# A three-product float32 transformer trunk: shorter GpSimd subtractions, moved diagonals, and VectorE's low halves in four operations

## What is computed

```python
for i in range(2):
    x = layer_norm(ALPHA * x + 0.5 * swiglu(x, ffn1_w_gu[i], ffn1_w_down[i]), ...)
    if i == 0: y, qm = gla_mix(x @ gla_w_in, ...);   w_out = gla_w_out
    else:      y, qm = conv_mix(x @ conv_w_in, ...); w_out = conv_w_out
    m = mem_attention(qm, mem, mem_w_kv[i])
    x = layer_norm(ALPHA * x + concatenate([y, m]) @ w_out, ...)
    x = layer_norm(ALPHA * x + 0.5 * swiglu(x, ffn2_w_gu[i], ffn2_w_down[i]), ...)
```

## Time and profile before

| | |
|---|---|
| median of 3 runs | 2048.76 us (2047.93 to 2050.04) |
| the profiled execution | 2046.01 us |
| its span, first to last instruction | 2044.3 us |
| TensorE busy / weight loads | 99% / 91% of the span |
| VectorE, ScalarE, GpSimd busy | 67%, 40%, 39% |
| granted TensorE clock, mean | 0.998 |
| HBM traffic | 215.8 MB read, 22.0 MB written, 116 GB/s |
| GpSimd, first feed-forward block | busy 8 to 9 tenths of slices 3 and 4 of 40 |

### The profile page before, as it was taken

One profiled execution on the slowest core, in us unless ns is written; L12 is line 12 of the kernel. 1 busy time (PEld: TensorE's weight loads), 2 busy tenths in 40 slices (PEclk: granted clock), 3 DMA queues, 4 the chain that ended last, 5 costly groups with the idle time before them and its releaser, 6 DMA issues.

```text
span 2044.3 us, 34286 instructions
## 1 busy us (share of the span) xinstructions
PE 2019.4 (99%) x13509; PEld 1853.8 (91%) x13509; DVE 1364.4 (67%) x1843; ACT 810.5 (40%) x1164; POOL 789.2 (39%) x444
## 2 busy tenths in 40 slices
PE   9999999999999999999999999999999899999998
PEld 9899998988988999999899999889887699999887
DVE  4477774554435768887456887646899886776645
ACT  5433452263433354444234444423453434434422
POOL 1499820033312258881015878001100335887000
PEclk9999999999999999999999999999999999999999
DMA  7545323332211234443232545233544322332232
GB/s 251 186 144 164 124 88 98 105 105 77 69 32 62 93 114 150 158 155 109 93 107 93 165 146 172 96 96 108 177 128 169 103 73 94 103 103 92 90 102 88
DMA packets 229513, 239.13 MB, mean 117 GB/s; under 512 B 5999, under 2 KB 222189, under 8 KB 227628
## 3 DMA queue, kind: packets, MB, share of 16 engines
q1 hardware_dynamic: 228780, 235.68, 35.4%
q10 hardware_dynamic: 640, 2.16, 0.3%
HBM read 215.80 MB, written 22.02 MB: 116 GB/s over the span
## 4 chain that ended last, share of the span: by engine, by line
PE 86%; POOL 4%; DVE 4%; issue 3%; ACT 2%; DMA 1%; DVEq 0%; SPq 0%; ACTq 0%; POOLq 0%
PE bank L1779 12%; PE bank L1780 12%; PE bank L1781 12%; PE bank L1908 10%; PE bank L1910 10%; PE bank L1909 10%; PE bank L1790 4%; PE bank L1791 4%; PE bank L1792 4%; PE bank L1862 1%; ACT whi L669 1%; POOL s L557 1%; POOL diag_tmp L589 1%; PE bank L1867 1%; PE bank L2210 1%
## 5 line engine op out<-in xcount | busy, mean ns | idle before, releaser
L669 ACT CAST whi<-raw 128x2048 fp32r<-128x2048 f32 (+3 forms) x191 | 324.0, 1697 | 875.2 <-POOL scratch L564 435.5
L1123 DVE TENSOR_TENSOR wlo<-raw,whi 128x2048 fp32r<-128x2048 f32 (+2 forms) x165 | 356.0, 2157 | 244.7 <-ACT whi L669 244.2
L541 POOL TENSOR_TENSOR tiny<-tiny 128x2 f32<-128x2 f32 (+1 forms) x13 | 9.4, 726 | 754.2 <-DVE tiny L1398 754.2
L560 POOL TENSOR_TENSOR raw<-raw 128x512 f32<-128x512 f32 x72 | 226.2, 3142 | 0.0
L1779 PE MATMUL bank<-h_hi,whi 128*128 128x512 f32 x528 | 207.1, 392 | 0.0
L1780 PE MATMUL bank<-h_lo,whi 128*128 128x512 f32 x528 | 205.5, 389 | 0.0
L1781 PE MATMUL bank<-h_hi,wlo 128*128 128x512 f32 x528 | 205.5, 389 | 0.0
L1908 PE MATMUL bank<-t_hi,whi 128*128 128x256 f32 x576 | 163.6, 284 | 2.8 <-DVE bank L1190 2.8
L564 POOL TENSOR_TENSOR scratch<-raw,s 128x512 f32<-128x512 f32 x72 | 149.2, 2073 | 39.7 <-DVE ex_lo L1130 39.7
L1908 PE MATMUL bank<-t_hi,ex_hi 128*128 128x256 f32 x576 | 163.8, 284 | 0.3 <-DVE ex_lo L1132 0.2
L1909 PE MATMUL bank<-xlo,whi 128*128 128x256 f32 x576 | 163.0, 283 | 0.0
(11 more groups left out here) (356 smaller groups left out, 5886.1 us busy)
## 6 DMA issues: line engine op xcount, KB each, us to landing
raw<-in_ffn_w_gu_dram SPq DMA_DIRECT2D x88, 1024.0 KB, 4.9
raw<-in_ffn_w_down_dram SPq DMA_DIRECT2D x32, 896.0 KB, 5.1
raw<-in_ffn_w_down_dram SPq DMA_DIRECT2D x32, 512.0 KB, 3.4
raw<-in_gla_w_in_dram SPq DMA_DIRECT2D x14, 1024.0 KB, 5.1
...
```

Of the source, the lines that this page charges most:

```text
L560: nc.gpsimd.tensor_tensor(a21, a21, a11, ALU.add).then_inc(w_sum, 1)
L669: nc.scalar.copy(whi[:, s, 0:kc, 0:width], raw[:, s, 0:kc, 0:width]).then_inc(hi_ready, 1)
L1123: nc.vector.tensor_tensor(wlo[:, s, 0:kc, 0:width], raw[:, s, 0:kc, 0:width], whi[:, s, 0:kc, 0:width].bitcast(F32), ALU.subtract).then_in ...
```

## The change

Five edits.
1. `lo_blocks`: GpSimd's subtractions outside the loops and weight sums (chunks GLA_N + 14 and + 15, the output projections' chunks, the spare parts, `b_lo_c`) go in blocks of 128x256, four or eight operations instead of one. In the convolution block two of the eight blocks of chunk CONV_OUT_N + 2 move ahead of `rsqrt`.
2. The diagonals: 0, 1, 2 ahead of the loop; 3, 4, 5 in passes 3, 5, 7; 6 and 7 behind it. SyncE's stores move accordingly, one between the two loads of a pass for passes 1 and 2. VectorE's wait for the stores moves to just before `residual_pair` of the first column pair.
3. The third memory chunk (n = 2) is cast and subtracted in two halves, and TensorE waits for each.
4. `r_evac(3)` goes ahead of `step(15)`.
5. In the first feed-forward block, passes 2 to 10, VectorE makes the low half of a full chunk in four operations of 128x512 back to back (`split_lo_quarters`); the semaphore counts after the last.

```diff
@@ -79,6 +79,7 @@
 GLU_EVAC = [2, 4, 6, 8, 14, 16, 18, 20]
 LATE = 3
 TAPS_K = [8, 8, 7, 7]
+DIAG_PAIR = [3, 5, 7]
 PE_TAPS = sum(TAPS_K)
 
 
...
@@ -342,13 +344,21 @@
...
                 n0 = FFN_N[f]
+
+                def diagonal_store(d):
+                    sp.wait_ge(diag_built, d + 1)
+                    sp.dma_start(diag_dram[d // 2, d % 2], diag_tmp[:, :, :].bitcast(F32)).then_inc(diag_stored, 16)
+
                 if f == 0:
                     for i in range(FK // 2):
                         load(n0 + 2 * i, 0, cols(w_gu, i * 256))
+                        if i in (1, 2):
+                            diagonal_store(2 * i - 2)
                         load(n0 + 2 * i + 1, 1, cols(w_gu, i * 256 + FF))
-                        if 0 < i <= 2 * len(TAPS_K):
-                            sp.wait_ge(diag_built, i)
-                            sp.dma_start(diag_dram[(i - 1) // 2, (i - 1) % 2], diag_tmp[:, :, :].bitcast(F32)).then_inc(diag_stored, 16)
+                        if i == 1:
+                            diagonal_store(1)
+                        if i - 1 in DIAG_PAIR:
+                            diagonal_store(3 + DIAG_PAIR.index(i - 1))
                 else:
                     def gate_and_up(i):
                         load(n0 + 2 * i, 0, cols(w_gu, i * 256))
@@ -387,7 +397,11 @@
                 if f in (1, 2):
                     sp.wait_ge(early_done, EARLY * f + 1)
                     early_store(EARLY - 1)
+                if f == 0:
+                    diagonal_store(6)
                 down_loads(0, (2, 3))
+                if f == 0:
+                    diagonal_store(7)
                 with sp.Fori(1, 4) as p:
                     down_loads(p, range(4))
 
@@ -510,6 +524,18 @@
 
         @block.gpsimd
         def _(pool):
+            def lo_blocks(to, whole, high, ks):
+                for k in ks:
+                    last = nc.gpsimd.tensor_tensor(to[:, k, :], whole[:, k, :], high[:, k, :].bitcast(F32), ALU.subtract)
+                return last
+
+            def split_lo_blocks(n, s, kc=8, after_dve=False):
+
+                pool.wait_ge(hi_ready, n + 1)
+                if after_dve:
+                    pool.wait_ge(lo_ready, n)
+                lo_blocks(wlo[:, s], raw[:, s], whi[:, s], range(kc)).then_inc(lo_ready, 1)
+
             def split_lo(n, s, kc=8, width=256, after_dve=False):
 
                 pool.wait_ge(hi_ready, n + 1)
@@ -524,8 +550,8 @@
                 for i in range(2):
                     pool.wait_ge(hi_ready, n0 + 4 + i + 1)
                     pool.wait_ge(lo_ready, n0 + 4 + i)
-                    nc.gpsimd.tensor_tensor(to[:, 1, A_K * i:A_K * i + A_K, :], raw[:, i, 0:A_K, :],
-                                            to[:, 0, A_K * i:A_K * i + A_K, :].bitcast(F32), ALU.subtract).then_inc(lo_ready, 1)
+                    lo_blocks(to[:, 1, A_K * i:A_K * i + A_K, :], raw[:, i], to[:, 0, A_K * i:A_K * i + A_K, :],
+                              range(A_K)).then_inc(lo_ready, 1)
 
             def lo_of(base, ks, tok, lo, hi):
                 for k in ks:
@@ -592,14 +618,16 @@
                         values[:, sum(TAPS_K[:g]):sum(TAPS_K[:g]) + kc, t:t + 1].to_broadcast([P, kc, P]), ALU.mult)
                 last.then_inc(diag_built, 1)
 
-            for i in range(PLAIN):
-                diagonal(i)
+            for d in range(3):
+                diagonal(d)
             pool.wait_ge(t_ready, 4)
             for i in range(PLAIN, FK // 2):
                 weight_sums(0, i, 0)
                 weight_sums(0, i, 1)
-                if i < 2 * len(TAPS_K):
-                    diagonal(i)
+                if i in DIAG_PAIR:
+                    diagonal(3 + DIAG_PAIR.index(i))
+            for d in (6, 7):
+                diagonal(d)
             norm(LN_FFN[0])
 
             nc.gpsimd.memset(att_mask, 1.0).then_inc(gla_masks, 1)
@@ -618,15 +646,15 @@
             with pool.Fori(1, 5) as i:
                 split_lo(GLA_N + 4 + 2 * i, 0)
                 split_lo(GLA_N + 5 + 2 * i, 1)
-            split_lo(GLA_N + 14, 0)
-            split_lo(GLA_N + 15, 1)
+            split_lo_blocks(GLA_N + 14, 0)
+            split_lo_blocks(GLA_N + 15, 1)
             pool.wait_ge(rms_var, 1)
             nc.gpsimd.tensor_tensor(rms_r, rms_v, minus_half, ALU.pow).then_inc(rms_rs, 1)
-            split_lo(GLA_OUT_N, 0, A_K)
-            split_lo(GLA_OUT_N + 1, 1, A_K)
-            split_lo(GLA_OUT_N + 3, 1, B_K, after_dve=True)
+            split_lo_blocks(GLA_OUT_N, 0, A_K)
+            split_lo_blocks(GLA_OUT_N + 1, 1, A_K)
+            split_lo_blocks(GLA_OUT_N + 3, 1, B_K, after_dve=True)
             spare_lo_parts(LN_GLA_OUT, GLA_OUT_N)
-            split_lo(GLA_OUT_N + 7, 1, B_K, after_dve=True)
+            split_lo_blocks(GLA_OUT_N + 7, 1, B_K, after_dve=True)
             norm(LN_GLA_OUT)
             all_weight_sums(1)
             norm(LN_FFN[1])
@@ -634,17 +662,20 @@
             norm(LN_FFN[2])
             nc.gpsimd.memset(conv_in[:, :, 0:PAD], 0.0).then_inc(conv_pad, 1)
 
+            pool.wait_ge(hi_ready, CONV_OUT_N + 3)
+            pool.wait_ge(lo_ready, CONV_OUT_N + 2)
+            lo_blocks(wlo[:, 0], raw[:, 0], whi[:, 0], range(2))
             rsqrt(LN_CONV, 0)
             pool.wait_ge(rstd_diag, UNIT[LN_CONV] + 1)
-            split_lo(CONV_OUT_N + 2, 0, B_K, after_dve=True)
+            lo_blocks(wlo[:, 0], raw[:, 0], whi[:, 0], range(2, B_K)).then_inc(lo_ready, 1)
             pool.wait_ge(raw_loaded[1], 16 * (CONV_OUT_N // 2 + 4))
             pool.wait_ge(mo_mm, 2 * HEADS)
             nc.gpsimd.tensor_copy(b_hi_c[:, :, :], raw[:, 1, :, :]).then_inc(b_hi_done, 1)
             pool.wait_ge(b_hi_done, 1)
             pool.wait_ge(w_used, DIAG_N + len(TAPS_K))
-            nc.gpsimd.tensor_tensor(b_lo_c[:, :, :], raw[:, 1, :, :], b_hi_c[:, :, :].bitcast(F32), ALU.subtract).then_inc(lo_ready, 1)
+            lo_blocks(b_lo_c, raw[:, 1], b_hi_c, range(8)).then_inc(lo_ready, 1)
             spare_lo_parts(LN_CONV_OUT, CONV_OUT_N)
-            split_lo(CONV_OUT_N + 7, 1, B_K, after_dve=True)
+            split_lo_blocks(CONV_OUT_N + 7, 1, B_K, after_dve=True)
             norm(LN_CONV_OUT)
             all_weight_sums(3)
             rsqrt(LN_FFN[3], 0)
@@ -898,7 +929,12 @@
             nc.scalar.copy(whi[:, 1, 4:8, :], raw[:, 1, 4:8, :]).then_inc(hi_ready, 1)
             for n in range(8):
                 act.wait_ge(w_used, n + 1)
-                split_hi(n // 2 + 1, n % 2)
+                if n == 0:
+                    act.wait_ge(raw_loaded[0], 32)
+                    nc.scalar.copy(whi[:, 0, 0:4, :], raw[:, 0, 0:4, :]).then_inc(third_hi, 1)
+                    nc.scalar.copy(whi[:, 0, 4:8, :], raw[:, 0, 4:8, :]).then_inc(hi_ready, 1)
+                else:
+                    split_hi(n // 2 + 1, n % 2)
                 for t in range(2):
                     c = n % 4
                     to = kv_t[:, n // 4, 2 * c + t, :] if c < 2 else kv_v[:, n // 4, t, (c - 2) * 256:(c - 1) * 256]
@@ -1017,9 +1053,12 @@
                 if h % 2 == 0:
                     step(12 + h // 2)
             for k in range(8):
-                if k in (0, 2):
-                    step(14 + k // 2, A_K)
-                    r_evac(2 + k // 2)
+                if k == 0:
+                    step(14, A_K)
+                    r_evac(2)
+                if k == 2:
+                    r_evac(3)
+                    step(15, A_K)
                 if k == 6:
                     split_hi(GLA_OUT_N // 2 + 1, 0, B_K)
                 act.wait_ge(y_ready, k + 1)
@@ -1123,6 +1162,15 @@
                 nc.vector.tensor_tensor(wlo[:, s, 0:kc, 0:width], raw[:, s, 0:kc, 0:width],
                                         whi[:, s, 0:kc, 0:width].bitcast(F32), ALU.subtract).then_inc(lo_ready, 1)
 
+            def split_lo_quarters(n, s):
+
+                dve.wait_ge(hi_ready, n + 1)
+                dve.wait_ge(lo_ready, n)
+                for k in range(0, 8, 2):
+                    last = nc.vector.tensor_tensor(wlo[:, s, k:k + 2, :], raw[:, s, k:k + 2, :],
+                                                   whi[:, s, k:k + 2, :].bitcast(F32), ALU.subtract)
+                last.then_inc(lo_ready, 1)
+
             def extra_lo(f, i, s):
 
                 q = summed(f, i, s)
@@ -1194,7 +1242,10 @@
                 n, last = FFN_N[f] + 2 * i, isinstance(i, int)
                 for step in range(3):
                     combine(f, i, 0, step)
-                split_lo(n + 1, 1)
+                if f == 0:
+                    split_lo_quarters(n + 1, 1)
+                else:
+                    split_lo(n + 1, 1)
                 combine(f, i, 0, 3)
                 extra_lo(f, i, 1)
                 if f in (1, 2):
@@ -1204,7 +1255,10 @@
                                             ALU.subtract).then_inc(early_done, 1)
                 for step in range(3):
                     combine(f, i, 1, step)
```

(26 more changed lines are left out.)

1 line of the change is left out of this document (added).

## The result

After: 2065.7 us median (2063.97 to 2068.68, 4 runs); before, on the same chip: 2049.4 us median (2047.93 to 2051.33, 4 runs). Ratio 1.0086, 95% interval 1.0074 to 1.0098: 0.9% slower. The profiled execution has a span of 2062.9 us against 2044.3.

The account below looks back on a forecast made before the run. TensorE's busy line (2019.4 of 2044.3 us) was taken as the bound. Terms 20.0 - 1.35 - 1.8 - 0.7 - 0.6 - 3.6 = +12.0 on 2046.0 gave 2058.0, plus 2.8 to the median: 2060.8 us, range 2044 to 2068.

Parts of the forecast that it names:

- Quarters: First feed-forward block: GpSimd's sums enter between VectorE's four operations, the load loop becomes the bound; net +20 us.
- steady halves: First feed-forward block, halves of a pass without diagonal or its store: nine cost 1.05 us each.
- disturbed half: First feed-forward block, half with a diagonal or its store: three sums enter; six cost 14.3 us together.
- diagonal 6 there costs nothing: Last pass of the first feed-forward loop: no sums left, so the low half still meets its deadline; 0 us.
- Rival A: First feed-forward block: VectorE keeps its turn through back to back quarters; faster, 2038.7 us; chance 0.14.
- Rival B: First feed-forward block: turns taken but loads come sooner; no change, some 2047 us; chance 0.14.
- x near zero: First feed-forward block: what GpSimd's operation still holds when VectorE's low half starts stays near zero.
- Waits behind L1242: TensorE's waits at 688 and 1650 us: VectorE no longer held behind GpSimd's long subtractions; -1.8 us.
- `c_lo`, variance: Convolution block: blocks end `c_lo` sooner, while two blocks ahead delay the variance steps; -3.6 us, bounds 0 and -6.2.
- `r_late`: `r_evac(3)` placed before the cast of 1.04 us removes TensorE's wait of 0.45 + 0.16; -0.6 us.
- kv chunk: Third memory chunk cast and subtracted in halves, so TensorE's idling for its low half goes; -1.35 us.
- stores: Diagonal stores moved on SyncE, possibly delaying load 13; 0 us, bounds 0 and +3.

Follow-up runs that it names:

- run 2: Kernel before, with only the quarters in the first feed-forward block added and six diagonals in the loop: 2076.6 us, ratio 1.0142.
- runs 3 and 4: Changed kernel: first, two low-half operations instead of four, 2054.8 us; second, quarters kept, GpSimd's third sum waiting for the low half in passes 3 to 10, 2052.1 us.
- run 6: Changed kernel without quarters, spare low parts and chunk before each output norm in one GpSimd operation in GLA and convolution blocks: 2043.5 us.
- run 7: Changed kernel without quarters, and without the two GpSimd blocks ahead of the convolution block's variance steps: 2042.1 us, ratio 0.9971.
- run 10: Same text as run 1, the changed kernel without quarters, timed again: 2044.7 us, ratio 0.9982.
- run 1: Changed kernel with each low half of the first feed-forward block again in one VectorE operation, other edits kept: 2044.1 us, ratio 0.9979.

## Why the prediction came out as it did

**Quarters: right, in its mechanism and nearly in its size.** The chain "load 5.0, two sums 2.7, low half 3.45, so 11.15 us against 10.08" is what the steady halves do (11.2), and three sums in a disturbed half give 5.76 us where I had worked out 5.85. What the sum overstated is the number of halves at full price: 17.65 us of waits, not 20. What it left out is the clock: two stretches at 1.2 GHz behind waits of 2 us, 3.0 us more. The two belong together: behind the stretches the halves wait nothing (206 us), 0.30 (217) and 1.09 (242.7), where their like wait 0.65 to 1.03 and 2.1, some 2.3 us less in all (an estimate from these waits), as in run 2. It also put the end of the loop at nothing ("diagonal 6 there costs nothing"), and forgot diagonal 7 there. That starts at 303.09, when diagonal 6 is stored, and enters VectorE's last low half and `h_lo` (the first takes 2.17 us instead of 0.68); TensorE waits 1.18 us at 308.95, which is in the 17.65. So +20.65 agrees with +20 in part by luck.

**Rival A** (quarters back to back keep the turn) fell in the first half with a queued sum: at 108 us L586 (issued at 108.26, 1.76 us) is served between the first quarter (108.19, 0.68 us) and the second, and those two take 2.38 us together instead of 1.28. **Rival B** (loads come sooner, x near zero) fell with 5.07 us from the last quarter to L583: a load comes no sooner than the buffer is free.

The Trainium skill (SBUF, "Who interferes with whom") calls the shared ports an exclusive lock, and says that whoever issues first gets them for a whole instruction. The traces agree, and runs 3 and 4 show what follows from it: what counts is how many of the other engine's instructions can be queued at a gap, and how many gaps there are. By the Trainium skill (VectorE: DVE Perf Modes, "The TRN2 errata") four quarters alone would take 2.76 us, an estimate from its (N+151)/0.96 ns for each; here they stand 0.60 apart, 2.49 in all (293.75 to 296.24, where nothing enters).

**Waits behind L1242: wrong.** The step said: "What waits for VectorE gains", -1.8 us, because one operation of 0.68 would no longer stand 4 us behind one of GpSimd's. That much came true: at 708 and 1668 us TensorE no longer waits for VectorE. But the step priced one VectorE operation behind one block, and didn't count two other things. First, GpSimd's own eight blocks pay turns (7.86 and 8.64 us instead of 5.6), and now TensorE waits for them, 0.25 us at 708 and 2.04 at 1668 (0.76 for VectorE at each before); I had bounded that at 1 us. It is the rule of the quarters once more, and I had applied it to them but not here. Second, blocks take longer even where nothing enters: 5.60 us against 4.61 for the chunk ahead of the GLA's spare parts. Its buffer is free that much later, so the load, the cast and the second spare part come later too, and meet VectorE's row at 690 us, which before began as the part ended. Run 6 shows that this meeting costs 1.5 us cut or whole: what is new is that they meet. I had put the low halves 1.2 us later, but asked only when TensorE needs them. Measured +2.4; run 6 shows 1.9 us of it gone with whole operations (0.41 + 0.61 + 0.32 + 0.57). No run made the chunk ahead whole again, so its share is read from the traces alone.

**`c_lo`, variance, `r_late`, kv chunk, stores: right** to 0.2 us each. `c_lo` with the variance steps gained 3.5 (3.6 said); the third chunk 1.25 (1.35); SyncE's order cost nothing: store 0 went at 61.62 as said, diagonal 1 started at 66.82 (I had store 0 land near 71), and load 13 was issued on time at 86.08. Apart from the two blocks ahead (run 7), none of these edits had a run of its own; which of the blocks bring `c_lo`'s gain is shown for the spare parts alone (1.07 us, run 6).

**The clock in the GLA block** (+1.6 at 650 us) isn't the change's. Of the twelve profiled executions of this study, six have such a stretch between 624 and 652 us and six have none, with and without quarters alike (run 10 has it, run 1, the same text, hasn't). One of 3.4 us near 450 or 470 us costs nothing: in the executions without it TensorE waits 1.2 to 1.4 us at 471 (place of run 1) instead. In runs 4 and 6 it lasts 6.8 us, and by that run 6 comes out 1.5 us behind run 1.

The forecast of 2060.8 is 4.9 us below the median of 2065.7, and inside its range. Of the 6.5 us by which the sum of spans fell short (18.5 against 12.0), 4.2 are the L1242 step, 4.6 the clock, and the block's waits give 2.35 back; the median stood less far from the profiled execution than before (1.1 us against 2.8), which hides a part of it.
